# Gate and up weights of the large expert items: column pairs replaced by whole rows, summed in seven PSUM banks

## The reference, cut to what matters

```
def swiglu(u, w_gate, w_up, w_down):
    return (jax.nn.silu(u @ w_gate) * (u @ w_up)) @ w_down

logits = (tok @ router).astype(jnp.float32)
top_v, top_i = lax.top_k(logits, 2)
w = jax.nn.softmax(top_v, axis=-1)
gates = jnp.sum(jax.nn.one_hot(top_i, 8) * w[..., None], axis=1)
for e in range(8):
    out = out + gates[:, e:e+1] * swiglu(tok, w_gate[e], w_up[e], w_down[e])
```

## Time and profile before

| | us |
|---|---|
| median of 3 runs (1268.42 to 1269.39) | 1269.29 |
| the profiled execution, its time | 1269.83 |
| the profiled execution, its span | 1268.1 |
| TensorE busy | 1234.1 |
| VectorE busy | 637.3 |
| ScalarE busy | 565.2 |

### The profile page before, as it was taken

The page is one execution under the profiler, slowest core; times in us unless marked ns, Lnnn a source line. Parts: engine busy times, 40 slices in busy tenths (PEclk is TensorE's granted clock), DMA queues, the critical chain, the costliest instruction groups (busy, mean ns, idle before and its releaser), DMA issues.

```text
span 1268.1 us, 18552 instructions
## 1 busy us (share of the span) xinstructions
PE 1234.1 (97%) x7266; PEld 875.2 (69%) x7266; DVE 637.3 (50%) x755; ACT 565.2 (45%) x871; POOL 99.5 (8%) x260
## 2 busy tenths in 40 slices
PE   9998999999999999999999999999999999999787
PEld 8988999999989944588853468884347887332232
DVE  6887765555765501488831168880226886010001
ACT  6665554443655511477730167770036775010001
POOL 1000000000000183100002100000310000110000
PEclk9999999999999999999999999999998999999999
DMA  9943544348533399999999999999999999999997
GB/s 329 373 139 129 199 173 173 122 166 264 194 117 117 134 425 428 403 412 416 428 423 426 421 407 415 416 426 423 428 407 412 415 424 384 423 429 423 426 429 293
DMA packets 89032, 424.48 MB, mean 335 GB/s; under 512 B 5457, under 2 KB 24050, under 8 KB 71282
## 3 DMA queue, kind: packets, MB, share of 16 engines
q1 hardware_dynamic: 88592, 422.76, 83.4%
q10 hardware_dynamic: 354, 0.54, 0.1%
HBM read 422.23 MB, written 1.05 MB: 334 GB/s over the span
## 4 chain that ended last, share of the span: by engine, by line
PE 87%; DMA 8%; DVE 2%; ACT 1%; SPq 1%; issue 1%; ACTq 0%; POOLq 0%; POOL 0%; DVEq 0%
PE psA L2067 9%; PE psY L2082 7%; PE psA L1694 7%; PE psB L2067 7%; PE psA L1696 7%; PE psA L1695 7%; PE psB L1694 7%; PE psB L1696 7%; PE psB L1695 7%; PE psY L1696 5%; PE psY L1695 5%; PE psY L1694 5%; DMA ring<-in_moe_w_gate 3%; DMA ring<-in_moe_w_up 2%; DMA ring<-in_moe_w_down 2%; PE psY L2035 1%
## 5 line engine op out<-in xcount | busy, mean ns | idle before, releaser
L1560 DVE TENSOR_TENSOR wlo<-ring,whi 128x2048 fp32r<-128x2048 f32 (+1 forms) x138 | 287.7, 2104 | 88.3 <-ACT whi L938 86.0
L938 ACT CAST whi<-ring 128x1024 fp32r<-128x1024 f32 x252 | 260.4, 1052 | 100.8 <-issue 34.6
L1307 DVE TENSOR_TENSOR wlo<-ring,whi 128x1024 fp32r<-128x1024 f32 (+2 forms) x104 | 152.3, 1484 | 19.4 <-ACT whi L754 19.3
L2067 PE MATMUL psA<-ring,resT 128*64 128x512 f32 x620 | 148.8, 597 | 13.2 <-DMA ring<-in_moe_w_gate 6.7
L754 ACT CAST whi<-ring 128x1024 fp32r<-128x1024 f32 (+1 forms) x134 | 133.4, 1023 | 60.4 <-PE psY L1696 28.2
L1625 DVE TENSOR_TENSOR rowbuf<-psY,rowbuf 128x512 f32<-128x512 f32 x28 | 18.6, 688 | 211.9 <-PE psY L2035 211.9
L2067 PE MATMUL psB<-ring,resT 128*64 128x512 f32 (+1 forms) x624 | 113.9, 486 | 0.0
L1694 PE MATMUL psA<-xhi,whi 128*128 128x256 f32 x368 | 105.0, 285 | 2.6 <-DVE wlo L1307 1.2
L1694 PE MATMUL psB<-xhi,whi 128*128 128x256 f32 x368 | 106.4, 289 | 0.0
L2067 PEld LDWEIGHTS psB<-ring,resT 128*64 128x64 f32 x624 | 44.9, 137 | 89.0 <-issue 89.0
L1695 PE MATMUL psA<-xlo,whi 128*128 128x256 f32 x368 | 102.8, 279 | 0.0
(11 more groups left out here) (364 smaller groups left out, 2148.3 us busy)
## 6 DMA issues: line engine op xcount, KB each, us to landing
ring<-in_moe_w_down SPq DMA_DIRECT2D x50, 2048.0 KB, 19.9
ring<-in_moe_w_gate SPq DMA_DIRECT2D x35, 1792.0 KB, 10.8
ring<-in_moe_w_up SPq DMA_DIRECT2D x32, 1792.0 KB, 17.7
ring<-in_moe_w_gate SPq DMA_DIRECT2D x18, 2048.0 KB, 20.1
ring<-in_moe_w_up SPq DMA_DIRECT2D x18, 2048.0 KB, 21.4
ring<-in_ffn_w_gate SPq DMA_DIRECT2D x5, 2048.0 KB, 7.8
ring<-in_ffn_w_up SPq DMA_DIRECT2D x5, 2048.0 KB, 8.0
ring<-in_ffn_w_down SPq DMA_DIRECT2D x5, 2048.0 KB, 7.9
```

The lines of the kernel that those rows point to most:

```text
L938: nc.scalar.copy(hi_of(NG + m, 2), item_part(ring, j, g, 2)).then_inc(hi_done, 2)
L1307: nc.vector.tensor_tensor(part_of(wlo, s, g, size), part_of(ring, s, g, size), f(hi_of(m, size)), ALU.subtract).then_inc(lo_done, size)
L1560: nc.vector.tensor_tensor(item_part(wlo, j, g, step), item_part(ring, j, g, step), f(hi_of(NG + m, step)), ALU.subtract).then_inc(lo_done, ...
L2067: ins = mm(few_bank(b)[half * FEW:(half + 1) * FEW, to:to + end - x], few_in[:, k, :], raw[:, x - q * W:end - q * W], start=k == 0, stop=k ...
```

## The change

Large items take gate and up in the layout that small items have: the list `few_slots` becomes the one `item_slots` for both kinds. For each of the 8 blocks of 128 input features one row of 7 cells comes in (14 KB of each matrix row), and each of its cells adds to a bank of its own; gate, and then up, has seven banks open at once (`big_bank`). The silus follow the last row of gate, column by column; the multiplications lie around the last row of up and in down; down is summed in `psA`. Chunks 0 and 1 are turned inside the last row of up, chunks 2 to 6 after down of the chunk two before. Since rows have 7 cells, the pieces that ScalarE and VectorE take are cut at row ends, at slot ends and at the 12 cells of `whi`: 92 casts in an item where there were 84, and 57 subtractions where there were 44. Small items now use their four banks in another order, and the large item's first two rows come in three pieces each (2, 2, 3 cells and 3, 2, 2) where the first two slots had four each.

```
-    item_slots = [("gate", 0, 1, 0), ("up", 0, 1, 0)]
-    for c in range(1, NE, 2):
-        item_slots += [(kind, c, 2, part) for kind in ("gate", "up") for part in range(2)]
-        item_slots += [("down", d, 1, 0) for d in range(max(c - 2, 0), c)]
-    item_slots += [("down", d, 1, 0) for d in range(NE - 2, NE)]
+    item_slots = [(kind, k) for kind in ("gate", "up") for k in range(KD)] + [("down", d) for d in range(NE)]
+    item_cells = [NE if kind != "down" else GS for kind, at in item_slots]
+    FIRST_PARTS = [[2, 2, 3], [3, 2, 2]]
...
+    HI_PIECES, LO_PIECES = split_pieces(2, 2), split_pieces(2, 4)
...
+        def big_bank(c):
+            return (psA[:, 0, :], psA[:, 1, :], psB[:, 0, :], psB[:, 1, :], psY[:, 1, :], psY[:, 2, :], psY[:, 0, :])[c]
...
             def expert(i):          # ScalarE
...
+                for c in range(NE):
+                    act.wait_ge(group_used, used_at(i, item_from[KD - 1] + c + 1))
+                    nc.scalar.activation(in_blocks(big_act(c)), by_block(big_bank(c)), ACT.Silu).then_inc(m_silu, 1)
+                    done = item_split(i, done, item_from[KD - 1] + c + 1 + AHEAD + 2)
+                for k in range(KD - 1):
+                    done = item_split(i, done, item_from[KD + k + 1] + AHEAD + 2)
+                done = item_split(i, done, 2 * CELLS + 4)
+                hidden_hi(i, 0)
+                done = item_split(i, done, 2 * CELLS + GS)
+                hidden_hi(i, 1)
...
             def expert(i):          # VectorE
...
+                for j in range(2 * KD - 1):
+                    done = item_halve(i, done, item_from[j + 1] + AHEAD)
+                multiply(i, 0)
+                multiply(i, 1)
+                done = item_halve(i, done, 2 * CELLS + 4)
+                hidden_lo(i, 0)
+                hidden_lo(i, 1)
...
+            def big_columns(i, j, kind, k):          # TensorE
...
+                for c in range(NE):
...
+                    if kind == "up" and k == 0:
+                        pe.wait_ge(m_silu, i * NE + (c + 1))
+                    three(big_bank(c), ihi[:, k, :], ilo[:, k, :], whi_of(NG + m), item_part(wlo, m, 1)[:, 0, :],
+                          k == 0, k == KD - 1).then_inc(group_used, 1)
+                    if kind == "up" and k == KD - 1 and 3 <= c < 5:
+                        hidden_turn(i, c - 3)
+            def big_down(i, j, c):
+                pe.wait_ge(m_hlo, hlo_at(i, max(c, 1)))
```

More of the change, by code:

```diff
@@ L159, in trunk @@
+    item_slot = {key: j for j, key in enumerate(item_slots)}
+    FS = len(item_slots)
+    item_cells = [NE if kind != "down" else GS for kind, at in item_slots]
+    item_from = [sum(item_cells[:j]) for j in range(FS)]
+    assert sum(item_cells) == IG and BANK_SUM[-1] == NE
     assert len(DOWN_ROWS) == NE and all(len(rows) == FBW for rows in DOWN_ROWS)
     MAX_ITEMS = E + 5
-    END_GATHER = [few_slot["down", 1], few_slot["down", 2]]
-    NEXT_SMALL_AT = few_slot["down", 6]
-    SUM_AT = {few_slot["up", 7]: (0, 1), few_slot["down", 3]: (1, 1), few_slot["down", 4]: (0, 0), few_slot["down", 5]: (1, 0)}
@@ L164, in trunk @@
[L164 to L170, removed]
+    END_GATHER = [item_slot["down", 1], item_slot["down", 2]]
@@ L171, in trunk, with split_pieces @@
+    NEXT_SMALL_AT = item_slot["down", 6]
+    SUM_AT = {item_slot["up", 7]: (0, 1), item_slot["down", 3]: (1, 1), item_slot["down", 4]: (0, 0), item_slot["down", 5]: (1, 0)}
+    BIG_GATHER = item_from[item_slot["down", NE - 2]]
+    SPREAD_AT = item_slot["up", 6]
+    SCATTER_AT = [item_slot[at] for at in (("gate", 7), ("up", 1), ("up", 5), ("up", 6))]
     CELLS = GS * RING
     AHEAD_CELLS = GS * AHEAD_SLOTS
+    BIG_FROM = GS * ((NS + SHIFT) % RING)
+    def split_pieces(first_size, size):
+        pieces, m = [], 0
+        for j in range(FS):
+            end = item_from[j] + item_cells[j]
+            while m < end:
+                n = min(first_size if j < 2 else size, end - m, HL - (NG + m) % HL, GS - (BIG_FROM + m) % GS)
+                pieces.append((m, n))
+                m += n
+        return pieces
@@ L1006, in result @@
                 for half, part in enumerate(parts):
-                    nc.scalar.copy(part, psY[:, 0 if few(i) else half, :]).then_inc(y_out, 2 // len(parts))
+                    nc.scalar.copy(part, psY[:, 0, :] if few(i) else psA[:, half, :]).then_inc(y_out, 2 // len(parts))
             def few_rows(i):
@@ L1553, in _, with item_halve @@
                     halve_to(end + AHEAD)
-            def item_halve(i, first, last, step=4):
-                for m in range(first, last, step):
-                    j, g = m // GS, m % GS
-                    dve.wait_ge(hi_done, split_at(i, m + step))
-                    nc.vector.tensor_tensor(item_part(wlo, j, g, step), item_part(ring, j, g, step),
-                                            f(hi_of(NG + m, step)), ALU.subtract).then_inc(lo_done, step)
+            def item_halve(i, done, last):
+                while done < len(LO_PIECES) and LO_PIECES[done][0] < last:
+                    m, size = LO_PIECES[done]
+                    dve.wait_ge(hi_done, split_at(i, m + size))
+                    nc.vector.tensor_tensor(item_part(wlo, m, size), item_part(ring, m, size),
+                                            f(hi_of(NG + m, size)), ALU.subtract).then_inc(lo_done, size)
+                    done += 1
+                return done
             def raw_lo(first, n):
@@ L2056, in few_columns @@
                         pe.wait_ge(rs_set, 1)
+                    if kind == "gate" and k == 0 and b == 2 and isinstance(i, int) and i:
+                        pe.wait_ge(y_out, 2 * i)
                     todo = []
@@ L2138, in _ @@
             for tb in range(TB):
-                ins = mm(psB[:, 1, 0:1], pick[:, tb, :], rstd[:, 0, tb:tb + 1], start=tb == 0, stop=tb == TB - 1)
+                ins = mm(psA[:, 0, 0:1], pick[:, tb, :], rstd[:, 0, tb:tb + 1], start=tb == 0, stop=tb == TB - 1)
             ins.then_inc(norm_mm, 1)
             def expert(i):
-                for j in range(IS):
-                    item_slot_products(i, j)
-                    for c in TURN_AFTER.get(j, []):
-                        hidden_turn(i, c)
+                for j, (kind, at) in enumerate(item_slots):
+                    if kind != "down":
+                        big_columns(i, j, kind, at)
+                        continue
+                    big_down(i, j, at)
+                    if at + 2 < NE:
+                        hidden_turn(i, at + 2)
             def start_sum(i, half, tb):
```

248 lines of the change are left out of this document (116 added, 132 removed).

## The result

The changed kernel takes 1272.07 us (median of 9 runs, 1271.2 to 1273.53), the kernel before, on the same chip, 1268.44 (9 runs). The ratio is 1.0027, with an interval of 1.0017 to 1.0036: 3.6 us slower, between 2.2 and 4.6. The forecast was 1272.0, and +2.7 us against the kernel before.

The account below looks back on a forecast made before the run. TensorE's end of item 5 plus a constant was taken to set the end, with the ring full. Old waits and clock -8.2, new waits +9.9, remaining starts +1.0 gave +2.7 us, forecast 1272.0; own range 1270 to 1275, overall 1263.5 to 1278.5.

Parts of the forecast that it names:

- What sets the end: The ring is full at item 5's end, so the kernel ends at TensorE's end of item 5 plus 193.7 us.
- costed at nothing: Longer rows save 2.6 us of transfer time per large item, 7.8 in all, but the full ring swallows it.
- the 8.2 us: All the change can win on TensorE's path: items 3 and 5 are 2.3 and 5.9 us longer than item 1.
- The waits of before: TensorE's waits of 2.04 us in item 3 and 3.04 in item 5, for low parts whose cast awaited a slot.
- kept for the starts: At the starts of items 3 and 5, 0.1 and 0.9 us of the waits stay, 1.0 us, bounds 0 and 2.
- the silus: After gate's last row in each large item, TensorE waits 0.6 us for cell 64, bounds 0.3 and 1.2.
- the first turn: In up's last row, TensorE waits 0.9 us for the multiplication, behind low parts of down's first four cells.
- down: Before the first cell of down, TensorE waits 1.8 us for the low parts of chunks 0 and 1.
- (a): Rival: the clock falls at the new handover too, 3.4 us per fall, one to three give 1275.4 to 1282; chance 0.22.
- (b): Rival: new waits are much shorter, say 1.2 us an item, as ScalarE and VectorE overlap more: 1265.2; chance 0.16.
- (c): Rival: transfers are the bound throughout and hide TensorE's new waits; 7.8 us come off, 1261.5; chance 0.10.
- (d): Rival: 14 KB rows run no faster in large items; 0.8 us more at the starts, 1272.8; chance 0.10.

Follow-up runs that it names:

- load in item 5: The kernel before with 12 extra float32 matmuls on TensorE in the middle of item 5: 1272.07 us, ratio 1.0023.
- short runs: The changed kernel with each gate and up row of large items, from the third on, in transfers of at most two cells: 1271.66 us, ratio 1.0025.
- halves: The kernel before with the third to sixth slot of each large item brought in as two transfers of four cells: 1267.73 us, ratio 0.9996.
- handover kernel: The changed kernel, chunks 0 and 1 multiplied before down's low parts and turned one column earlier, chunk 1 rounded after one weight-cast pair: 1263.98 us, ratio 0.9963.
- multiplications first: The changed kernel with VectorE's multiplications of chunks 0 and 1 ahead of the low parts of down's first four cells: 1269.01 us, ratio 1.0004.
- handover kernel with short runs: The handover kernel with each gate and up row of large items, from the third on, in transfers of at most two cells: 1268.07 us, ratio 0.9995.
- load in item 6: The kernel before with the same 12 extra matmuls on TensorE near the start of item 6, a small one: 1268.53 us, ratio 1.0000.

## Why the prediction was right, point by point

**What sets the end.** Right for the two kernels compared, and shown: load in item 5 counts, in item 6 it doesn't. The forecast's "costed at nothing" for the long rows was right for this change (short runs cost the changed kernel nothing). What the forecast didn't say is how near the other bound was. It took the 8.2 us as what relief gives; halves, which take away one of the two waits, part of the other and the fall of the clock, give 0.7 us with the transfers of before. In the changed kernel the relief counted with long rows and with short ones alike, because the new waits brought TensorE back to about where it had been. Only a kernel relieved on balance, like the handover kernel, needs the long rows for it. So a reader of the forecast would have overrated a change that only removes the waits. By the rule of the Trainium skill, DMA: Bandwidth & Descriptors, section Specifications, that 512 B reach line rate, the two handover kernels would take the same time; 411 and 426 GB/s and 4.1 us say otherwise.

**The waits of before.** Gone, and the granted clock is 1.00, as forecast. In the sum 1.0 us was kept for the starts; 1.4 came, all in item 5 (1.24 in the trace), none in item 3.

**The new waits.** All three at their places and with their releasers. Against the pitch: the silus 0.46 us (forecast 0.6), the first turn 0.88 (0.9), down 1.40 (1.8), together 2.7 an item against 3.3. The steps of the chain, counted from the start of up's last row at 602.70: turn at 3.68 (3.7), first rounding at 4.37 (4.4), second at 6.75 (6.8). The last wait came out too long by terms on both sides: ScalarE hands over to VectorE in 0.03 us (610.07 behind 609.45 + 0.59) where 0.1 was taken, VectorE to TensorE in 0.05 (610.81 behind 610.07 + 0.69) where 0.15 was taken from one row, and the two turns hold TensorE 0.93 us (606.38 to 609.41 less three cells of 0.70) instead of 0.72, so that TensorE itself was ready at 6.7 and not at 6.5. These are sizes; the mechanism stood. Runs with one and with both waits taken away gave back 3.1 and 8.1 us.

**The sum.** Forecast -8.2 + 9.9 + 1.0 = +2.7. With the sizes measured, the same terms give -8.2 + 8.2 + 1.4 = +1.4. Measured on TensorE by items, 124.3, 124.4 and 125.8 us against 121.4, 123.7 and 127.3, it is +2.1: each large item has another 0.2 us beside its waits. With the starts of the items between, item 6 starts 2.0 us later. Behind that point the span has another 1.0 us, which gives the 3.0 of the spans; the last 0.6 us of the 3.6 between the medians are there because the profiled execution of before lay 1.4 us above its median and the changed one's 0.8. So the forecast's own terms carry 1.4 of the 3.6 us. That it met the median so exactly is luck, in two places: new waits taken too long by 1.7 us stood for things not in the sum, and the 2.7 us were added to a median of 1269.29 from three executions, where nine gave 1268.44. Why another 1.0 us comes behind item 5 is open. The changed kernel's transfers are held up harder there (1056 to 1076 us: 351 GB/s against 380 in the earlier trace rows; the piece of 0.8 MB landed in 6.7 us against 7.5), so less may be on its way when item 6 begins; by the windows 79.1 x 419 + 94.0 x 425 = 73.1 MB still came in from there on, against 72.9 before, which would be 0.5 us. But short runs in the same kernel gave 193.9 between, and one execution of each doesn't settle it.

**The rivals.** (a) The clock didn't fall at the new handover. (b) Shorter waits: by 0.6 us an item, far from 1.2 in all. (c) Transfers as the bound throughout: refuted for the kernel before by the load in item 5 and for the changed one by the multiplications first, but transfers do set the end in the kernel with halves and in the handover kernel with short runs. (d) Rows of 14 KB are faster in large items: 426 against 411 GB/s. The copy out of psA before the next small item's third bank cost nothing, as no such wait stands in the trace. Three slips of the texts changed nothing: (b)'s sum keeps 0.5 us at the starts where the forecast keeps 1.0 (1265.7, not 1265.2); with a bit over half of the forecast's and (d)'s cases above 1271.8, slower comes to about 0.49, not 0.44; and the kernel before made 46 subtractions in a large item (16 cells in eight of two, 152 in 38 of four), not 44, so the change adds 11, as the windows show (67 and 68 against 56 and 57), not 13.

## What to carry to other kernels

When two resources are both near 100% busy, ask at one point in time which of them is being held up (a buffer full, a rate equal to the consumer's, landings shorter than those of equal transfers elsewhere), and then how far the other is behind: a relief is worth only that distance, and an edit that is worth nothing alone (here the long rows) can be worth 4 us behind another. When an operand's work is moved to the end of a stage, follow the queues of the engines that hand it over: what stands ahead of the small urgent operation (a cast of weights, a subtraction for later) is what the consumer waits for, and putting the urgent one first cost nothing here. An order that hid a handover behind other work loses that cover when the work is regrouped.

## What the runs showed that I had not expected

The clock's answer to nearly the same wait differs between executions of the same stage. The kernel before and the one with load in item 6, which are the same up to there, wait 3.04 and 2.97 us at the start of item 5, and the windows of 960 to 970 us show a granted clock of 0.66 and 0.83 (last column but two). The one with load in item 5 waits 1.77 us and shows 1.00; in the kernel with halves it is 1.00 after 2.57 us. The kernel before:

```profile
960.00:970.00 10.00, 8.43 (x25) 6.71 (x26) 8.15 (x5) 6.06 (x6) 0.00 (x0) 0.66 1.04 417
```

With load in item 6:

```profile
960.00:970.00 10.00, 8.86 (x34) 7.12 (x35) 8.67 (x6) 6.64 (x8) 0.00 (x0) 0.83 1.05 422
```

With load in item 5:

```profile
960.00:970.00 10.00, 8.23 (x38) 6.68 (x38) 9.72 (x7) 8.10 (x10) 0.00 (x0) 1.00 1.04 416
```

So of the 8.2 us up to 3 were of that one execution's clock, and item 5 may end up to 3 us later in it than in another execution of the same kernel: with load in item 6, item 6 starts at 1072.8 us instead of 1074.3, and the transfers are held up less before it (423 GB/s from 1045 to 1065 us, against 399). In the executions of the kernel before the mean granted clock is mostly 0.997, where the profiled one has 0.996. The profile that the forecast read was thus a slower execution than most, and the other bound was nearer than it showed.
